# Two narrow projections merged into one unit of 36 columns, with the forget gate's chain and the decoding scores issued later

## The reference

```
h = x + 0.5 * post1(SwiGLU1(pre1(x)))                   # feed-forward, 2816 wide
u = preM(h);  P = u @ w_in                              # one combined input projection
[A | B | C | D] = Conformer conv | GLA | short gated conv | forgetting attention
h = h + postM(concat(A, B, C, D) @ w_out)
h = h + 0.5 * post2(SwiGLU2(pre2(h)))
```

```
log_a = log_sigmoid(a_lr @ w_a2 + b_a) / 16             # a_lr: 16 columns of P
S_t   = exp(log_a) * S_(t-1) + k v                      # GLA, in chunks of 64
logf  = log_sigmoid(P[4 columns] + b_f)                 # D
score = q k / 8 + cumsum(logf)_q - cumsum(logf)_k       # causal softmax over the prompt
decode: softmax over 256 cached rows (paged keys, values, logf) and the new one
```

## Time and profile before

| | |
|---|---|
| median of three executions | 1093.97 us |
| the profiled execution | 1094.53 us |
| its span, first to last instruction | 1092.7 us |
| TensorE matmuls busy | 1064.1 us, 97% |
| TensorE weight loads | 1028.8 us, 94% |
| VectorE | 705.6 us, 65% |
| ScalarE | 550.6 us, 50% |
| GpSimd | 274.5 us, 25% |
| mean granted TensorE clock | 0.993 |
| read from HBM | 182.40 MB, 170 GB/s over the span |

### The profile page before, as it was taken

One profiled execution on the slowest core, in us unless ns is written; L12 is line 12 of the kernel. 1 busy time (PEld: TensorE's weight loads), 2 busy tenths in 40 slices (PEclk: granted clock), 3 DMA queues, 4 the chain that ended last, 5 costly groups with the idle time before them and its releaser, 6 DMA issues. The chain is left out here.

```text
span 1092.7 us, 24133 instructions
## 1 busy us (share of the span) xinstructions
PE 1064.1 (97%) x8956; PEld 1028.8 (94%) x8956; DVE 705.6 (65%) x1045; ACT 550.6 (50%) x887; POOL 274.5 (25%) x340
## 2 busy tenths in 40 slices
PE   6999999989999999999999999999899999999997
PEld 5999999988879999999999999998888899999997
DVE  5666644589995766654476665436999776666443
ACT  6544454554357644454474445446534675444542
POOL 3222221304504322220132223012053042222200
PEclk9999999999999999999999999999999999999999
DMA  7666677342726566656646666763426257656561
GB/s 269 207 186 180 179 222 232 98 155 79 232 78 196 155 193 180 184 166 187 188 127 203 180 180 188 232 186 117 139 79 209 79 190 217 180 179 176 178 181 53
DMA packets 63747, 186.92 MB, mean 171 GB/s; under 512 B 9515, under 2 KB 19763, under 8 KB 63539
## 3 DMA queue, kind: packets, MB, share of 16 engines
q1 hardware_dynamic: 63666, 185.81, 56.2%
HBM read 182.40 MB, written 3.38 MB: 170 GB/s over the span
## 5 line engine op out<-in xcount | busy, mean ns | idle before, releaser
L313 DVE TENSOR_TENSOR w_lo<-raw,w_hi 128x1024 fp32r<-128x1024 f32 (+1 forms) x316 | 411.1, 1306 | 332.0 <-ACT w_hi L303 331.8
L303 ACT ACTIVATE w_hi<-raw 128x1024 fp32r<-128x1024 f32 x336 | 342.9, 1026 | 283.0 <-PE ub L345 188.4
L343 PE MATMUL ub<-hg_hi,w_hi 128*128 128x264 f32 x960 | 278.7, 290 | 6.3 <-DVE proj L1315 6.3
L344 PE MATMUL ub<-hg_lo,w_hi 128*128 128x264 f32 x960 | 274.9, 286 | 0.0
L345 PE MATMUL ub<-hg_hi,w_lo 128*128 128x264 f32 x960 | 274.6, 286 | 0.0
L343 PE MATMUL ub<-act_hi,w_hi 128*128 128x264 f32 x704 | 200.5, 285 | 0.0
L345 PE MATMUL ub<-act_hi,w_lo 128*128 128x264 f32 x704 | 200.0, 284 | 0.0
L344 PE MATMUL ub<-act_lo,w_hi 128*128 128x264 f32 x704 | 199.1, 283 | 0.0
L343 PE MATMUL quad<-hg_hi,w_hi 128*128 128x264 f32 x688 | 196.4, 285 | 0.0
L344 PE MATMUL quad<-hg_lo,w_hi 128*128 128x264 f32 x688 | 194.9, 283 | 0.0
L345 PE MATMUL quad<-hg_hi,w_lo 128*128 128x264 f32 x688 | 194.8, 283 | 0.0
(11 more groups left out here) (252 smaller groups left out, 1314.4 us busy)
## 6 DMA issues: line engine op xcount, KB each, us to landing
raw<-in_w_gu SPq DMA_DIRECT2D x176, 512.0 KB, 4.1
raw<-in_w_dn SPq DMA_DIRECT2D x64, 512.0 KB, 4.1
raw<-in_w_in SPq DMA_DIRECT2D x44, 512.0 KB, 3.8
raw<-in_w_dn SPq DMA_DIRECT2D x32, 384.0 KB, 3.7
raw<-in_w_out SPq DMA_DIRECT2D x16, 512.0 KB, 3.7
pages<-in_cache_k SPq DMA_DIRECT2D x32, 128.0 KB, 3.3
pages<-in_cache_v SPq DMA_DIRECT2D x32, 128.0 KB, 3.1
con<-in_con SPq DMA_DIRECT2D x1, 1448.0 KB
```

Of the source, the lines that this page charges most:

```text
L303: eng.activation(w_hi[:, slot, 0:w], raw[:, slot, 0:w], ACT.Copy).then_inc(*sig("hi_ready", reps))
L313: eng.tensor_tensor(w_lo[:, slot, 0:w], raw[:, slot, 0:w], w_hi[:, slot, 0:w].bitcast(F32), ALU.subtract)\
L343: eng.matmul(out, a_hi, x_hi[:, k0 + k, :], start=(first and k == 0), stop=False)
L344: eng.matmul(out, a_hi, x_lo[:, k0 + k, :], start=False, stop=False)
```

## The change

The two narrow units become one of 36 columns: 16 of the low-rank gate on partitions 0 to 15 of the result, 4 of the forget gate on partitions 32 to 35 (`FG_ROWS`), zeros between. The phase has 23 units of weights (`IN_UNITS`); its last place in the ring is left empty, so the counts of the ring are corrected (`empty_turns`, `no_unit`, `counted`). The following units move up by one number. `mix` is called with the step of the new count plus one, so most of the mixers' work stays behind the same weights as before; GpSimd splits units 13 to 22. Tiles and constants of the forget gate lie on partitions 32 to 35.

Two things do not keep their place. ScalarE's softplus of the forget gate moves from step 2 to step 7 and VectorE's part of that chain from step 3 to step 9. TensorE's `decode_scores` move from step 15 to step 16, and so behind `gla_outputs` and one more unit. SyncE's `mix` keeps its steps. The core of the diff (left out are shapes, the calls of `mix` with one more, and waits on `proj` whose number is one less):

```
@@ -55,8 +55,10 @@
 COLS = KD * P
 
 
-ALR, FG, BQ, BK, AG, BG, AV, BV, DQ, DKK, DVV, CC, CX, CB = 0, 1, 2, 3, 4, 6, 8, 10, 12, 14, 16, 18, 19, 22
-IN_WIDTH = [16, 4] + [P] * 22
+ALR, FG, BQ, BK, AG, BG, AV, BV, DQ, DKK, DVV, CC, CX, CB = 0, 0, 1, 2, 3, 5, 7, 9, 11, 13, 15, 17, 18, 21
+IN_UNITS = 23
+FG_ROWS = slice(32, 36)
+IN_WIDTH = [FG_ROWS.stop] + [P] * (IN_UNITS - 1)
 
 
 RING = 4
...
@@ -220,11 +222,26 @@
             return con[0:part, CON[name]:CON[name] + cols]
 
         ident, ones, blk = const("ident", P), const("ones", P), const("blk", P)
+        sel = con[FG_ROWS, CON["sel"]:CON["sel"] + H * P]
 
         def tile_of(tiles, n):
 
             return tiles[:, n, :] if isinstance(n, int) else tiles[:, bass.ds(n, 1), :].rearrange("p a c -> p (a c)")
 
+
+        def no_unit(phase, idx):
+
+            return phase == "in" and idx == IN_UNITS
+
+        def counted(phase, idx):
+
+            return 2 if phase == "in" and idx == IN_UNITS - 1 else 1
+
+        def empty_turns(layer, phase, slot):
+
+            if slot != IN_UNITS % RING:
+                return 0
+            return layer + (phase in ("out", "gu1", "dn1"))
 
         def steps(eng, phase, l, body, pattern=4, peel_first=False):
...
@@ -271,13 +288,14 @@
         def turn_before(lead):
 
             if lead["phase"] == "out" and lead["index"] < RING:
-                return "in", lead["index"] + PHASES["in"][1] - RING
+                back = lead["index"] + PHASES["in"][1] - RING
+                return "in", back if back < IN_UNITS else back - RING
             return lead["phase"], lead["index"] - RING
 
         def pooled_just_before(lead):
 
             if lead["phase"] == "out":
-                return len(POOLED) if lead["index"] == 0 else 0
+                return len(POOLED) + PHASES["in"][1] - IN_UNITS if lead["index"] == 0 else 0
             return 0
 
         def load_unit(eng, lead, reps):
...
@@ -466,7 +485,7 @@
                         if phase == "dn0":
                             load_past(l, s)
                         if phase == "in":
-                            mix(l, s)
+                            mix(l, s + 1)
                         if phase == "gu1" and isinstance(i, int) and i == 0:
                             store_states(l, s)
                     steps(sp, phase, l, turn, 24 if phase == "dn0" else PATTERN[phase], peel_first=phase == "gu1")
...
@@ -620,10 +639,10 @@
                 mm.then_inc(*sig("a_var"))
 
             def fox_scores(l, h):
-                after(l, d_qm=2, d_cf=2, proj=16, b_rs=2, b_og=3)
+                after(l, d_qm=2, d_cf=2, proj=15, b_rs=2, b_og=3)
                 for out, q0, n in ((fox_bank[h][:, 0:P], 0, P), (fox_bank[h][:, P:3 * P], P, TP)):
                     pe.matmul(out, qm[:, h, q0:q0 + P], proj[:, DKK + h // 2, 0:n], start=True, stop=False)
-                    mm = pe.matmul(out, const("sel", H * P, H)[:, h * P:(h + 1) * P], cf[:, 0:n], start=False, stop=True)
+                    mm = pe.matmul(out, sel[:, h * P:(h + 1) * P], cf[:, 0:n], start=False, stop=True)
                 mm.then_inc(*sig("d_sc"))
 
             def fox_transposes(l, h):
...
@@ -693,7 +712,7 @@
 
             def mix(l, n):
 
-                if n == 3:
+                if n == 4:
                     after(l, proj=1)
                     pe.matmul(mb[2][:, 0:NT], par[0:16, PAR["wa2"]:PAR["wa2"] + P], proj[0:16, ALR, :], start=True, stop=True).then_inc(*sig("b_z"))
                 if 5 <= n <= 11:
@@ -703,9 +722,10 @@
                 if n == 13:
                     gla_updates(l)
                 if n == 15:
+                    gla_outputs(l)
+                if n == 16:
                     decode_scores(l, 0)
                     decode_scores(l, 1)
-                    gla_outputs(l)
                 if n == 17:
                     decode_new(l)
                     gla_norm(l)
@@ -717,7 +737,7 @@
                     fox_scores(l, 3)
                 if n == 20:
                     decode_back(l)
-                    after(l, proj=18, d_sm=4)
+                    after(l, proj=17, d_sm=4)
                     transposes(mb[2], proj[:, DVV:DVV + 2, :], "d_vT")
                 if n == 21:
                     conv_sum(l)
...
@@ -736,16 +756,16 @@
                 multiply_first(pe, l, "in", hg_hi, hg_lo, ub, IN_WIDTH, "hg_ready", 0)
                 pe.wait_ge(*at(l, "h_acc", 9))
                 pe.matmul(NORM, ones, h_acc[:, :], start=True, stop=True).then_inc(*sig("h_sum"))
-                for n in range(GROUP, 24):
+                for n in range(GROUP, IN_UNITS):
                     if pooled("in", n):
                         pe.wait_ge(*at(l, "rest_half", pool_count(n)))
                     else:
                         pe.wait_ge(S["split_done"], l * UNITS + PHASES["in"][0] + n + 1 + RING)
                     if n >= 4:
                         pe.wait_ge(*at(l, "proj", {4: 1, 5: 2}.get(n, n - 1)))
-                    multiply_unit(pe, unit_bank(n)[:, 0:NT], n % RING, hg_hi, hg_lo, KD, 0, True, True, 1)
-                    mix(l, n)
-                pe.wait_ge(*at(l, "proj", 24))
+                    multiply_unit(pe, unit_bank(n)[:, 0:NT], n % RING, hg_hi, hg_lo, KD, 0, True, True, 1, count=counted("in", n))
+                    mix(l, n + 1)
+                pe.wait_ge(*at(l, "proj", IN_UNITS))
                 pe.wait_ge(*at(l, "d_pt", 4))
                 multiply_first(pe, l, "out", ym_hi, ym_lo, ub, [P] * GROUP, "ym_ready", 0)
                 for n in range(GROUP, KD):
...
@@ -862,14 +882,14 @@
                 if n == 4:
 
                     after(l, b_z=1)
-                    softplus(l, soft[:, :], mb[2][:, 0:NT], par[:, PAR["ba"]:PAR["ba"] + 1], "b_sp")
-                if n == 2:
+                    softplus(l, soft[:, :], mb[2][:, 0:NT], par[:, PAR["ba"]:PAR["ba"] + 1], biases[:, 2:3], "b_sp")
+                if n == 7:
+
+                    after(l, proj=1)
+                    softplus(l, lft[:, :], proj[FG_ROWS, FG, :], par[FG_ROWS, PAR["bf"]:PAR["bf"] + 1], biases[FG_ROWS, 2:3], "d_sp")
+                if n == 3:
 
                     after(l, proj=2)
-                    softplus(l, lft[:, :], proj[0:H, FG, :], par[0:H, PAR["bf"]:PAR["bf"] + 1], "d_sp")
-                if n == 4:
-
-                    after(l, proj=3)
                     act.activation(proj[:, BQ, :], proj[:, BQ, :], ACT.Copy, scale=DK ** -0.5).then_inc(*sig("b_qs"))
                 if n == 5:
                     after(l, b_bc=2)
@@ -880,7 +900,7 @@
                 if n == 8:
 
                     act.preload_act_table(ACT.Sigmoid)
-                    after(l, proj=8)
+                    after(l, proj=7)
                     act.activation(proj[:, AG:AG + 2, :], proj[:, AG:AG + 2, :], ACT.Sigmoid).then_inc(*sig("a_sg"))
                     act.activation(sg[:, :, :], proj[:, BG:BG + 2, :], ACT.Sigmoid).then_inc(*sig("b_sg"))
                     act.preload_act_table_set("natural_log_exp_and_others")
...
@@ -1115,12 +1134,12 @@
                             dve.scalar_tensor_tensor(out, x, w, y, ALU.mult, ALU.add).then_inc(*sig("a_tap"))
 
             def mix(l, n):
-                if n == 3:
-
-                    after(l, d_sp=3, proj=2)
-                    log_sigmoid(l, lf[:, :], proj[0:H, FG, :], par[0:H, PAR["bf"]:PAR["bf"] + 1], lft[:, :], "d_lf")
+                if n == 9:
+
+                    after(l, d_sp=3, proj=1)
+                    log_sigmoid(l, lf[:, :], proj[FG_ROWS, FG, :], par[FG_ROWS, PAR["bf"]:PAR["bf"] + 1], lft[:, :], "d_lf")
                     after(l, d_lf=2)
-                    dve.tensor_tensor_scan(cf[:, 0:TP], const("ones", TP, H), lf[:, 0:TP], 0.0, ALU.mult, ALU.add).then_inc(*sig("d_cf"))
+                    dve.tensor_tensor_scan(cf[:, 0:TP], con[FG_ROWS, CON["ones"]:CON["ones"] + TP], lf[:, 0:TP], 0.0, ALU.mult, ALU.add).then_inc(*sig("d_cf"))
                     after(l, d_cf=1)
                     dve.tensor_scalar(cf[:, 0:TP], cf[:, 0:TP], -8.0, None, ALU.mult).then_inc(*sig("d_cf"))
                 if n == 4:
...
@@ -1319,17 +1338,15 @@
                         rest_unit(dve, lead, reps)
                     if s == 1:
                         dve.wait_ge(*at(l, "rh_ready", 4))
-                    if s == 12:
+                    if s == 11:
                         after(l, b_sc=7, b_msk=6)
                     if s >= 1:
                         evacuate(s - 1)
-                    mix(l, s)
+                    mix(l, s + 1)
                     if s > GROUP:
                         rest_unit(dve, lead, reps)
-                    behind(l, s)
+                    behind(l, s + 1)
                 steps(dve, "in", l, inp, 24)
-                evacuate(23)
-                mix(l, 24)
                 for first in (YC, YD, YA):
                     rest_mixed(l, first)
                 steps(dve, "out", l, lambda i, s, reps, lead: rest_unit(dve, lead, reps), 8)
...
@@ -1519,16 +1536,20 @@
```

(10 more changed lines are left out.)

137 lines of the change are left out of this document (76 added, 61 removed).

## The result

The changed kernel takes 1113.55 us, median of 4 runs (1112.81 to 1115.91); the kernel before takes 1093.97. The ratio is 1.0178, with a 95% interval of 1.0165 to 1.0191. Forecast were 1103.5 us and a range of 1094 to 1109, so the sign was right, the size was half of what was measured, and the time lies outside the range. The profiled execution took 1113.77 us. From layer to layer the output norm's sums start at 358.12 us against 348.20 before, and at 904.33 against 885.08: 9.9 us are lost in the first layer and 9.3 in the second.

What follows compares the result with a forecast made beforehand. It took TensorE, busy 97%, as the bound, VectorE as second, and SyncE's queue as third. Delays of 4.5 and 5.0 us in the two layers made 9.5 us, 1103.5 us against the median of 1093.97; range 1094 to 1109.

Steps and rivals of the forecast that it cites:

- SyncE's queue decides: Mixer's input projection: late decoding scores hold value loads and weights behind them; TensorE waits some 9 us for ScalarE's squares.
- the second: Rival: the values' loads do not hold TensorE and VectorE's lead is kept, 1085 or 1088.2 us; chance 0.12.
- the first: Rival: same stall before the group norm's sums, but no further slow clock, 1098.5 us; chance 0.25.
- VectorE's lead of 4.5 us: Input projection: VectorE reaches the thirteenth unit's evacuation 4.5 us sooner, with bounds of 2.6 and 6 us.
- The early wait: Early input projection: TensorE's wait of 3.17 us was to shrink to near 2 us, now for the first mask.
- The release at 277.7: Layer 0: SyncE's queue starts the values' loads at 277.7 us, 4.7 us later than before.
- The clock after the wait, +1.0 us: TensorE's first unit after the 9 us wait runs partly at 1.2 GHz: 1.0 us, with bounds 0 and 2.9.
- From there to the output projection VectorE is busy without a break, and nothing gives the time back.: After the fourth head's biased scores, the delay of 4.5 us in layer 0 was to stay in full.
- the sum had 9.5: Both layers together: attention scores end 4.5 us later in layer 0 and 5.0 in layer 1.
- Rival four: Attention scores also at half clock through the first two heads, 2 us or more a layer, 1108 us; chance 0.13.

Runs made afterwards that it cites:

- The scores back: Changed kernel with only the decoding scores put back in front of the GLA outputs: 1093.41 us, ratio 0.9978.
- the scores late in the kernel before: Kernel before with only the decoding scores one unit later, behind the GLA outputs: 1121.72 us, ratio 1.0232.
- the run with the late loads: Changed kernel, decoding scores left late, with SyncE's loads of past values two turns later, three a turn: 1102.12 us, ratio 1.0065.
- both edits: Changed kernel with decoding scores back before the GLA outputs, and third output unit's rounding and remainder ahead as in the kernel before: 1086.39 us, ratio 0.9925.
- the chain's move alone: Kernel before with only the forget gate's chain moved, ScalarE's part from place 2 to 7, VectorE's from 3 to 9: 1089.05 us, ratio 0.9941.
- the merged unit alone: Changed kernel with decoding scores, third output unit's preparation and forget gate's chain at their old places: 1091.82 us, ratio 0.9985.
- the edit that mends it: Changed kernel with only ScalarE's third output-unit rounding ahead of its waiting steps and VectorE's remainder ahead of the last evacuation: 1106.93 us, ratio 1.0102.

## Why the prediction was wrong, step by step

- *SyncE's queue decides.* Right. The scores back give 20.1 us, the scores late in the kernel before cost 26.3, and with more weights issued ahead of the wait the squares come 12.5 us earlier. Of the rivals, the second (TensorE isn't held) is out by the wait of 9.0 us, the first by the clock. The late place of the scores costs little beside the queue: 0.8 us in layer 0 of the run with the late loads; in layer 1 of that run some 5 us stay unexplained.
- *VectorE's lead of 4.5 us.* 4.2 from the phase's mark, in the changed kernel and with both edits. The size was right, its parts were not: of 4.5 us the prediction put 3.0 down to the chain's move and 1.5 to the merged unit; the chain's move alone gives 4.5, and the merged unit alone 0.2. That the sum of the parts came out near was luck.
- *The early wait.* Forecast near 2 us and for the first mask. It was 2.56, for the evacuation of a unit whose bank level 0 writes, and 1.10 more stood behind the moved chain. No slow unit followed it in this execution (230.27 to 233.16, 2.9 us).
- *The release at 277.7.* 278.71, 1.0 us later: 0.4 because the phase began later in this execution, 0.3 from the lead, 0.2 from the slow unit (4.6 us where 4.4 were reckoned), 0.1 from the rest. The distance from there to the squares' end held: 12.7 against 12.5.
- *The clock after the wait, +1.0 us.* It was +2.55 in layer 0. The term was bounded by 0 and 2.9 and the lower part was chosen, with the reason that part of the slow stretch would fall into the wait. But the clock was at 0.50 for the end of the wait and for five to six us of work behind it; the wait did not use the slow stretch up. The near row was a wait of 3.17 us with 1.5 us lost; for a wait three times as long the lower part of the bounds had no row to stand on. The run with 20 added matmuls gives it back. Together with the later release this is why the fourth head's scores ended 7.4 and not 4.5 us late (6.8 and not 5.0 in layer 1); 0.4 of the 7.4 is the later beginning of the phase.
- *"From there to the output projection VectorE is busy without a break, and nothing gives the time back."* Half right: VectorE was busy without a break from 309.18 to that point, yet 1.2 us were given back in each layer, since the start of the output projection is 330.98 against 324.80. Then the sum ended, and this is the step that failed: nothing was put down for what lies behind the start of the output projection. The seam behind it costs 2.1 us of wait and about 1.6 us of slow clock in each layer; the edit that mends it gives 6.6 us (7.0 with the scores back). It was to be read from the order of ScalarE's instructions: the last three roundings before the output projection and the steps that wait between them.
- *Where the missing time was.* The spans differ by 19.3 us where the sum had 9.5. Of the 9.8 us between them, 4.7 are the later end of the attention scores (2.9 and 1.8 in the two layers), -2.4 what was given back behind it, and 7.5 the seam, for which the prediction had no term.
- *Rival four's slow attention scores.* Its 1108 us came nearer, but for another reason than it gave: the four heads took 11.2 us, as before (308.45 + 0.69 - 297.94).

By the measured parts: -7.6 (what is left with both edits), +6.6 or 7.0 (the seam, with the scores late or not), +20.1 or 20.5 (the scores' place, with the seam as it is or mended), which makes 19.6. That such a sum closes is arithmetic. What shows them to be two causes is that each stays without the other: with the scores back TensorE still waits 1.97 us at the seam, and with the seam mended it still waits 8.75 us for the squares. With a term for the seam the forecast would have been 7 us higher, some 1110, and with the clock's term at its far end some 1114. The range was too narrow because it had the bounds of the clock's term, and no term at all for a place behind the point where the sum stopped.

## What to carry to other kernels

When a phase loses a unit of work, look at its seam: what runs ahead by a fixed number of places in the ring (loads, roundings) counts an empty place as well, so what it prepares for the next phase comes one step later against the rest of the work. The place to look is the first instruction in the helper engine's order that waits for the end of the phase. A wait in a DMA queue is paid by what stands behind it in that queue, here weights; so before a producer is moved later, count the transfers behind its consumer. And a sum over the parts of a change is finished only at the end of the span, not where the last wait was seen.

## What the runs showed of the hardware

In the changed kernel TensorE's clock fell late in the long wait and came back late in the work. After its last matmul near 282.6 us it still was granted full speed to 286; 0.69 in 286 to 288; then 0.50, to the end of the wait and through the first 4.5 us of matmuls; 0.75 in 296 to 298. The price of this wait of 8.92 us stood behind it, 2.55 us. The Trainium skill ("TensorE: Matmul & The Clock Gate", section "HAM oscillation — how this bites in real kernels") tells of waits between groups of matmuls after which the next group starts cold; behind this wait the windows agree, with 0.50 at the start of the next group.

Behind shorter waits the next group began at full speed here and slowed down afterwards: about 1 us into the unit behind the 3.17 us of the kernel before, and about 0.6 us into the work behind the 1.97 us at the seam. The same wait of 2.56 us before level 0 was followed by a unit of 2.9 us in the changed kernel and by one of 4.0 us in the version with only the seam mended (231.32 to 235.32).

Work that nobody reads can be worth its place in such a wait: 20 matmuls of 256 columns in it made the kernel 3.1 us faster. The unit behind the GLA outputs runs at 0.50 in the changed kernel although TensorE doesn't wait there, as it did before; what precedes it are narrow matmuls (64 columns, then 2), but no run tested them as the cause. In the version with the scores back and the seam mended it does not, in layer 0 (272 to 288 at 1.00), and slow stretches stand among the attention scores instead (0.50 from 290 to 294 and again from 300 to 302). Which unit pays moves from version to version, and a version's time moves with it by a few us.
